# Ending the matrix memory inside the RWKV context features, and joining the features to the scan

## The chip, the core and the metric

The kernel runs on one core of a Trainium2 chip. The metric is device time in microseconds (us): the median of three runs of the kernel before is 2667.61 us (2666.59 to 2672.57).

## What is computed

One layer of a diffusion backbone: two token mixers on the same normalised input (a bidirectional RWKV-7 scan and a bidirectional chunkwise mLSTM, the "matrix memory"), a gated merge, and a PEER expert FFN. 512 latent tokens are computed, and 256 context tokens before them whose final states start the latent scans. The parts that the change touches:

```python
# mLSTM: the end of its output (both directions z, 4 heads of 128)
h = num / jnp.maximum(jnp.abs(den), jnp.exp(-m_row))[..., None]
h = h * rsqrt(mean(h * h, -1) + NORM_EPS) * mlstm_norm_g     # per head and direction
y = jnp.sum(h, axis=directions)
# RWKV: what the scan reads
decay = exp(-exp(w_log));  a = sigmoid(a0 + ad @ a_up)
kk = k * k_k / max(norm(k * k_k), 1e-12);  k_eff = k * (1 + (a - 1) * k_a)
S = S * w_t - s_kk (kk_t * a_t) + v_t k_t                    # 8 heads of 64 x 64
```

## The kernel before

The program is a row of blocks. Between two blocks all engines meet; inside one, every engine runs its own list of instructions, in the order in which they are written, and waits on semaphores. The blocks around the change, in order:

- `phase_mlstm` (the matrix memory): TensorE makes products per chunk of 128 tokens, ScalarE and VectorE gather them in `hc`. Its end handles the norms. VectorE makes the reciprocal of each denominator (L1746 to L1748, `den_done`), GpSimd multiplies the chunk by it (L1492, `divided`), ScalarE squares it (L1633), VectorE sums the squares (L1732). After the last of the eight, ScalarE makes Ln and Exp of all sums (L1654, L1656), GpSimd scales direction 1 (L1495, four times 128x512), VectorE scales direction 0 (L1754) and adds the two (L1757), TensorE turns the 16 tiles of 128x128 (L1606), and ScalarE and VectorE evict two heads each (L1659, L1760).
- `phase_rwkv_features` for the context (names ending in `_c`, 256 tokens), then later for the latent tokens (`_x`, 512 tokens). There are eight units n = (direction z, column tile c), four per direction. For each, TensorE makes two projections (`project`, L596 and L598), ScalarE makes the decay's tanh, the rate's tanh and the decay's exp (L569, L571, L577), for direction 1 also `ke` (L582; GpSimd makes it for direction 0, L615). VectorE makes a running product over each chunk of 64 with `tensor_tensor_scan` (`decay`, L638) and the rates (`rates`, L649). After unit 2, ScalarE also makes Ln and Exp of the four norms of `kk` (L586, L588). The decay buffer `w65` has 65 columns per chunk: direction 0 has its reset column in front and direction 1 behind, so VectorE rewrites it between the directions (L666), after the fourth scan, and ScalarE waits for that (`slot_done`) before the exp of the fifth unit.
- `phase_rwkv_scan`, again for the context and then for the latent tokens: a hardware loop over chunks of 64 tokens, the two directions g = 0 and 1 side by side. `prepare` on GpSimd makes `pr` (L772, L775), `ks` (L777) and, after VectorE's reciprocal `ginv` (`inverse`, L991), `qs` and `ks` (L782). The first products on TensorE (L915) read these: "Q0" and "Q1" below are those of the first chunk with `qs` of direction 0 and 1, 16 records each. VectorE's second reciprocal waits for GpSimd's first `prepare`, since the semaphore's count is started behind it (`start`, L69).

The order of the work is the order of the code; no planner decides anything. After the latent scan follow output, merge, routing and experts, which all begin behind a meeting of the engines.

In the text a "unit" is one of the eight of the features, counted from 1; "the last unit's end" is the end of L582 of unit 8.

Of the kernel before, what the change touches and what calls it, by code (L numbers as in the profile page):

```python
# [12 lines left out]
F32 = mybir.dt.float32  # L13
# [519 lines left out]
def phase_rwkv_features(nc, a, b, f, T, tag):  # L533

    nch = T // C
    with ExitStack() as ctx:
# [8 lines left out]
        w65 = sb("w65" + tag, [P, PAIRS, nch, C + 1])  # L545
        first = sb("w65_first" + tag, [P, nch, C + 1])
        tmp = sb("rw_tmp" + tag, [P, PAIRS, T])
        th = sb("rw_th" + tag, [P, 2, T])
        ps = [ctx.enter_context(nc.psum_tensor(f"ps_rf{k}" + tag, [P, 512], F32)) for k in range(4)]
        ps_n = [ctx.enter_context(nc.psum_tensor(f"ps_rn{k}" + tag, [P, 512], F32)) for k in range(PAIRS)]  # L550
# [4 lines left out]
        dve, scanned, slot_done, normed = sem("rwf_dve"), sem("rwf_scanned"), sem("rwf_slot"), sem("rwf_normed")  # L555
        line_pool, line_act = sem("rwf_line_pool"), sem("rwf_line_act")
        block = ctx.enter_context(nc.Block())
        units = [(z, c) for z in range(2) for c in range(PAIRS)]

        @block.scalar  # L560
        def _(act):
            act.activation(f[0:64, 12, :], f[0:64, 12, :], ACT.Tanh).then_inc(tanh_wd, 1)
            for c in range(PAIRS):
                act.wait_ge(sq_in, c + 1)
                act.activation(tmp[:, c, :], b.kk[:, c, 0:T], ACT.Square).then_inc(sq_done, 1)
            act.wait_ge(half_done, 1)
            for n, (z, c) in enumerate(units):
# [16 lines left out]
                if n == 1:  # L584
                    act.wait_ge(norm_max, 1)
                    act.activation(tmp[:], tmp[:], ACT.Ln).then_inc(norm_root, 1)  # L586
                    act.wait_ge(norm_root, 1)
                    act.activation(tmp[:], tmp[:], ACT.Exp, scale=-0.5).then_inc(norm_root, 1)  # L588

        @block.tensor  # L590
        def _(pe):
# [15 lines left out]
            for n in range(2, len(units)):  # L607
                project(n)

        @block.gpsimd  # L610
        def _(g):
            g.wait_ge(half_done, 1)
            for c in range(PAIRS):
                g.wait_ge(a_done, c + 1)
                g.tensor_scalar(b.ke[:, 0, c, 0:T], b.qa[:, 0, c, 0:T], ka[:, 0, c:c + 1], ka[:, 1, c:c + 1], ALU.mult,  # L615
                                ALU.add).then_inc(line_pool, 1)

        @block.vector
        def _(v):
# [8 lines left out]
            v.memset(w65[:, :, :, 0:1], 0.0).then_inc(slot_done, 1)  # L628

            def decay(n):  # L630
                z, c = units[n]
                v.wait_ge(dec_done, n + 1)
                w = w65[:, c].rearrange("p n t -> p (n t)")
# [17 lines left out]

            for c in range(PAIRS):
                v.wait_ge(norm_mm, c + 1)
                m = v.tensor_scalar(tmp[:, c, :], ps_n[c][:, 0:T], 1e-24, None, ALU.max)
# [10 lines left out]
            v.wait_ge(scanned, PAIRS)  # L665
            v.memset(w65[:, :, :, C:C + 1], 0.0).then_inc(slot_done, 1)  # L666
            v.wait_ge(slot_done, 2)
            for n in range(2, PAIRS):
                rates(n)
            for n in range(PAIRS, 2 * PAIRS):  # L670
                decay(n)
                rates(n)

def phase_rwkv_scan(nc, a, b, f, T, tag, need_out):
# [11 lines left out]
    with ExitStack() as ctx:  # L687
# [10 lines left out]
        pr, ginv = each("pr", [P, PAIRS, RW]), each("ginv", [P, PAIRS, C])  # L698

        pd, qs, ks, vs, lt, mt = (each(n, [P, PAIRS, C]) for n in ("pd", "qs", "ks", "vs", "lt", "mt"))  # L700
        qt, kt, ti, td, xd = (each(n, [P, PAIRS, C]) for n in ("qt", "kt", "ti", "td", "xd"))
        at, bt, vv, ro = (each(n, [P, PAIRS, C]) for n in ("at", "bt", "vv", "ro"))
        rr, uu, st, tm = (each(n, [P, PAIRS, C]) for n in ("rr", "uu", "st", "tm"))
# [18 lines left out]
        gi_s = [Steps(sem(f"rws_gi{g}"), ["gi"]) for g in range(2)]  # L722
# [3 lines left out]
        block = ctx.enter_context(nc.Block())  # L726
# [28 lines left out]
        def _(g_):  # L755
            def prepare(n, g, first=False):
# [2199 lines left out]
```

## Time and profile before

| | us |
|---|---|
| median of 3 runs | 2667.61 |
| the profiled execution, whole | 2667.66 |
| its span in the profile | 2665.9 |
| last instruction of the matrix memory ends | 332.73 |
| context features, first instruction to the last unit's end | 334.03 to 352.74 |
| context scan, "Q0" and "Q1" begin | 358.40, 362.14 |
| latent features, first instruction | 468.72 |
| latent scan, "Q0" and "Q1" begin | 504.09, 508.75 |

The profile is one execution. Its timeline has a row for an instruction or for a few equal ones in a row, with start, duration, engine, line, and in brackets the idle time of the engine before it and what ended it. Overlap is seen by comparing starts: an instruction on ScalarE or VectorE starts some 0.1 us before the one ahead of it has ended.

### The profile page before, as it was taken

What the parts mean: (1) busy time and instruction counts of PE and PEld (TensorE: products, weight loads), DVE (VectorE), ACT (ScalarE), POOL (GpSimd) and SP (SyncE); (2) the same over time, 40 slices, a digit from 0 to 9 for tenths busy, and PEclk for the clock granted to TensorE, in tenths of its full rate; (3) what the DMA queues carried; (4) which work ended last, traced back from release to release, by engine and by line L of the source; (5) the groups of instructions that cost most, each with busy time, mean ns of one, the idle gap of its engine ahead of it and who ended that gap; (6) DMA issues with size and microseconds to landing.
All of it is one profiled execution on the core that took longest, in us unless ns stands there. A gap on an engine that the chain in (4) does not pass through costs nothing.

```text
span 2665.9 us, 53106 instructions
## 1 busy us (share of the span) xinstructions
PE 2519.4 (95%) x19732; PEld 2078.4 (78%) x19732; DVE 1309.2 (49%) x2662; ACT 1020.5 (38%) x1725; POOL 850.1 (32%) x689
## 2 busy tenths in 40 slices
PE   7999669699999989999999999989999999999997
PEld 3885469499967867887888888878888888888886
DVE  5765655656553327997444444400044444444443
ACT  4222453533352233223666666632322322232222
POOL 2420243444554445645555555524400000000001
PEclk8999889799999999999999999999999999999999
DMA  6541000000032324234355444464455555555551
GB/s 263 188 174 40 1 2 1 2 0 0 1 145 89 94 71 143 85 100 144 115 205 181 169 169 169 169 236 142 134 196 197 190 189 189 191 196 196 194 197 64
DMA packets 163913, 348.64 MB, mean 131 GB/s; under 512 B 13368, under 2 KB 79416, under 8 KB 161664
## 3 DMA queue, kind: packets, MB, share of 16 engines
q1 hardware_dynamic: 163840, 347.65, 37.7%
q8 instruction: 48, 0.79, 0.1%
q14 instruction: 25, 0.20, 0.0%
HBM read 276.30 MB, written 71.30 MB: 130 GB/s over the span
## 4 chain that ended last, share of the span: by engine, by line
PE 53%; DVE 5%; issue 1%; DMA 1%; POOL 1%; ACT 1%; SPq 0%; DVEq 0%; ACTq 0%; POOLq 0%
PE ps_a L85 9%; PE ps_a L86 9%; PE ps_a L87 9%; PE ps_y L85 7%; PE ps_y L86 7%; PE ps_y L87 7%; PE ps_w L2535 4%; DVE cand L2328 0%; DVE top_ix L2311 0%; DMA w_scratch<-w_block 0%; DVE top_ix L2324 0%; DVE scores_left L2314 0%; DVE picked L2385 0%; DVE pick L2369 0%; DVE pick L2152 0%
## 5 line engine op out<-in xcount | busy, mean ns | idle before, releaser
L2711 DVE TENSOR_TENSOR v_lo<-v_raw,v_hi 128x1024 fp32r<-128x1024 f32 x128 | 158.3, 1237 | 542.2 <-ACT v_hi L2663 542.2
L85 PE MATMUL ps_a<-h_hi,u_hi 128*128 128x512 f32 x1024 | 412.0, 402 | 8.2 <-ACT act L2056 7.7
L86 PE MATMUL ps_a<-h_hi,u_lo 128*128 128x512 f32 x1024 | 405.7, 396 | 0.0
L87 PE MATMUL ps_a<-h_lo,u_hi 128*128 128x512 f32 x1024 | 405.7, 396 | 0.0
L2663 ACT ACTIVATE v_hi<-v_raw 128x1024 fp32r<-128x1024 f32 x128 | 135.8, 1061 | 478.4 <-PE ps_a L87 470.0
L85 PE MATMUL ps_y<-gated_hi,v_hi 128*128 128x512 f32 x768 | 299.5, 390 | 3.1 <-DVE gated_lo L2713 3.1
L87 PE MATMUL ps_y<-gated_lo,v_hi 128*128 128x512 f32 x768 | 299.3, 390 | 0.0
L86 PE MATMUL ps_y<-gated_hi,v_lo 128*128 128x512 f32 x768 | 299.2, 390 | 0.0
L2056 ACT ACTIVATE act<-ps_a 128x512 f32<-128x512 f32 x128 | 76.5, 597 | 414.0 <-PE ps_a L87 397.4
L85 PEld LDWEIGHTS ps_a<-h_hi,u_hi 128*128 128x128 f32 x1024 | 194.0, 189 | 52.4 <-issue 8.5
L2699 POOL TENSOR_TENSOR v_raw<-v_raw 128x512 f32<-128x512 f32 x6 | 7.7, 1288 | 711.7 <-ACT v_raw L2683 711.7
L87 PEld LDWEIGHTS ps_a<-h_lo,u_hi 128*128 128x128 f32 x1024 | 193.4, 189 | 46.0
L86 PEld LDWEIGHTS ps_a<-h_hi,u_lo 128*128 128x128 f32 x1024 | 193.9, 189 | 43.1
L2516 POOL TENSOR_SCALAR mixed<-iota,w_token 128x128 f32<-128x128 f32 x128 | 151.4, 1183 | 218.2 <-PE ps_w L2535 202.4
L2040 POOL TENSOR_TENSOR u_lo<-u_raw,u_hi 128x1024 fp32r<-128x1024 f32 x64 | 156.3, 2445 | 181.6 <-ACT u_hi L2036 181.6
L2040 DVE TENSOR_TENSOR u_lo<-u_raw,u_hi 128x1024 fp32r<-128x1024 f32 x64 | 78.5, 1226 | 251.4 <-ACT u_hi L2036 251.4
L85 PEld LDWEIGHTS ps_y<-gated_hi,v_hi 128*128 128x128 f32 x768 | 144.5, 188 | 33.5 <-DVE v_lo L2711 3.5
L87 PEld LDWEIGHTS ps_y<-gated_lo,v_hi 128*128 128x128 f32 x768 | 144.5, 188 | 30.1
L86 PEld LDWEIGHTS ps_y<-gated_hi,v_lo 128*128 128x128 f32 x768 | 144.5, 188 | 30.0
L2036 ACT ACTIVATE u_hi<-u_raw 128x1024 fp32r<-128x1024 f32 x128 | 134.4, 1050 | 40.8 <-DMA u_raw<-in_uT 40.8
L2567 ACT ACTIVATE w_block<-ps_w 128x512 f32 x128 | 141.2, 1103 | 0.0
L1077 POOL TENSOR_TENSOR mg_w_lo<-mg_raw,mg_w_hi 128x1024 fp32r<-128x1024 f32 x38 | 94.0, 2475 | 126.9 <-ACT mg_w_hi L1073 126.9
(524 smaller groups left out, 5417.4 us busy)
## 6 DMA issues: line engine op xcount, KB each, us to landing
u_raw<-in_uT SPq DMA_DIRECT2D x128, 512.0 KB, 3.6
v_raw<-in_v SPq DMA_DIRECT2D x128, 512.0 KB, 4.8
a_scratch<-act SPq DMA_DIRECT2D x128, 256.0 KB, 2.1
w_scratch<-w_block SPq DMA_DIRECT2D x8, 4096.0 KB, 12.2
w_ring<-w_scratch SPq DMA_DIRECT2D x64, 512.0 KB, 4.4
gated<-a_scratch SPq DMA_DIRECT2D x128, 256.0 KB, 4.8
mg_raw<-in_w_merge SPq DMA_DIRECT2D x36, 512.0 KB, 3.6
vM<-in_ada_rows SPq DMA_DIRECT2D x32, 512.0 KB, 4.9
```

The source lines that it names most:

```text
L85: pe.matmul(out, wh, xh, start=first, stop=False)
L86: pe.matmul(out, wl, xh, start=False, stop=False)
L87: return pe.matmul(out, wh, xl, start=False, stop=last)
L1077: g.tensor_tensor(self.wl[:, k], self.raw[:, k], self.wh[:, k], ALU.subtract).then_inc(self.w_lo, 1)
L2036: act.activation(self.uh[:, q], self.raw[:, q % 2], ACT.Copy).then_inc(self.hi, 1)
L2040: eng.tensor_tensor(self.ul[:, q], self.raw[:, q % 2], self.uh[:, q], ALU.subtract).then_inc(self.lo, 1)
L2056: act.activation(self.act[:, q % 2], self.ps[q % 2][:], ACT.Gelu).then_inc(self.out, 1)
L2516: g_.tensor_scalar(oi[:, s, SUB - 1], iota, cur[:, s, 0:1], cur[:, s, 1:2], ALU.is_equal, ALU.mult).then_inc(built_p, 1)
L2535: m = pe.matmul(ps[s][:, k, :], oi[:, s, k], oj[:, s, k], start=True, stop=True)
L2567: act.activation(wb[:, half, :, bass.ds(g * BODY + dt, SUB)].rearrange("p j t -> p t j"), ps[s][:], ACT.Copy).then_inc(evac[s], 1)
L2663: act.activation(vh[:, q], v_raw[:, q], ACT.Copy).then_inc(v_hi, 1)
L2711: v.tensor_tensor(vl[:, q], v_raw[:, q], vh[:, q], ALU.subtract).then_inc(v_lo, 1)
```

## The change

1. `phase_mlstm` ends after its last reciprocal. The last two divisions (GpSimd), the last two squares (ScalarE) and sums (VectorE), Ln and Exp, the scaling, the adding, the turning and the evictions are moved into the context features. There ScalarE, and no longer VectorE, scales direction 0, in 16 instructions of 128x128; GpSimd still scales direction 1.
2. `w65` exists once per direction, so no rewriting and no wait between the directions.
3. Features and scan are one block, for the context and for the latent tokens. The scan's first reciprocals become four small ones (128x64) per direction, made between the scans and rates of units 5 to 8. GpSimd's first `prepare` waits on the features' semaphores per direction, and "Q" waits for `qs` alone, where it waited for `ks` too.

```diff
 # phase_rwkv_features, ScalarE
+            if end is not None:
+                for z in range(2):
+                    act.wait_ge(end.divided, z + 1)
+                    act.activation(square[:, z], outer(z), ACT.Square).then_inc(end.squared, 1)
...
-                if z == 1:
-
-                    act.wait_ge(slot_done, 2)
-                act.activation(w65[:, c, :, 1:] if z == 0 else w65[:, c, :, 0:C],
+                act.activation(w65[0][:, c, :, 1:] if z == 0 else w65[1][:, c, :, 0:C],
...
                     act.activation(tmp[:], tmp[:], ACT.Ln).then_inc(norm_root, 1)
+                    if end is not None:
+                        act.wait_ge(end.reduced, 2)
+                        act.activation(end.ssq[:], end.ssq[:], ACT.Ln, bias=b.eps[:, 0:1], scale=1.0 / DV).then_inc(
+                            end.rooted, 1)
...
+                        for i in range(n_x):
+                            for h in range(MH):
+                                m = act.activation(y[:, 0, i, h * DV:(h + 1) * DV], hc[:, 0, i, h, 0:DV], ACT.Copy,
+                                                   scale=end.ssq[:, 0, i, h:h + 1])
+                            m.then_inc(end.scaled0, 1)
+                if n == PAIRS and end is not None:
+                    act.wait_ge(end.turned, 1)
+                    for h in range(MH // 2, MH):
+                        act.activation(b.yb[:, h, :].rearrange("p (r w) -> p w r", w=GRID_W),
+                                       ps_n[h][:].rearrange("p (w r) -> p w r", r=ROWS), ACT.Copy, scale=end.gain[:, h:h + 1])
 # TensorE
             for n in range(2, len(units)):
+                if n == PAIRS and end is not None:
+                    pe.wait_ge(norm_max, 1)
+                    for i in range(n_x):
+                        pe.wait_ge(end.summed, i + 1)
+                        for h in range(MH):
+                            mm = pe.transpose(ps_n[h][:, i * MC:(i + 1) * MC], y[:, 0, i, h * DV:(h + 1) * DV], b.ident[:])
+                    mm.then_inc(end.turned, 1)
                 project(n)
 # GpSimd
+                if c == 1 and end is not None:
+                    g.wait_ge(end.rooted, 2)
+                    g.wait_ge(end.divided, 2)
+                    for i in range(n_x):
+                        g.tensor_tensor(y[:, 1, i].rearrange("p (h v) -> p h v", v=DV), hc[:, 1, i, :, 0:DV],
+                                        end.ssq[:, 1, i].unsqueeze(2).to_broadcast([P, MH, DV]), ALU.mult).then_inc(
+                                            end.scaled1, 1)
 # VectorE
             for n in range(2, PAIRS):
                 decay(n)
-            v.wait_ge(scanned, PAIRS)
-            v.memset(w65[:, :, :, C:C + 1], 0.0).then_inc(slot_done, 1)
-            v.wait_ge(slot_done, 2)
             for n in range(2, PAIRS):
                 rates(n)
+            if end is not None:
+                for i in range(n_x):
+                    v.wait_ge(end.scaled0, i + 1)
+                    v.wait_ge(end.scaled1, i + 1)
+                    v.tensor_tensor(y[:, 0, i], y[:, 0, i], y[:, 1, i], ALU.add).then_inc(end.summed, 1)
...
             for n in range(PAIRS, 2 * PAIRS):
                 decay(n)
+                m = inverse(0, n - PAIRS)
...
                 rates(n)
+                if n == PAIRS and end is not None:
+                    v.wait_ge(end.turned, 1)
...
+                m = inverse(1, n - PAIRS)
...
 # phase_rwkv_scan, GpSimd, then TensorE
+                if first:
+                    g_.wait_ge(entry.scanned, (g + 1) * PAIRS)
+                    g_.wait_ge(entry.normed, (g + 1) * PAIRS)
+                    g_.wait_ge(entry.line_act if g else entry.line_pool, PAIRS)
...
+                        prep_s[g].wait(pe, i, "k" if k else "q")
                         if k == 0:
-                            prep_s[g].wait(pe, i, prep_names[-1])
```

What moves, in rows of each engine's list (line numbers are those of the kernel that is listed). TensorE, from the end of the matrix memory to the projections of the context's third unit, before:

```order
L1589 MATMUL ps_mu<-vM,ml_kw_x 64x129 x2
L1606 MATMUL ps_ms<-ident,mixed 128x128 x2
L1606 MATMUL ps_me<-ident,mixed 128x128 x2
L1431 UNCONDITIONAL_BRANCH
L590 UNCONDITIONAL_BRANCH
L596 MATMUL ps_rf_c<-fC,wa_up 128x256
L598 MATMUL ps_rf_c<-fC,wa_up 128x256
L606 MATMUL ps_rn_c<-rw_tmp_c,block_ones 128x256 x4
```

and in the changed kernel, from the norms of `kk` on:

```order
L648 MATMUL ps_rn_c<-rw_tmp_c,block_ones 128x256 x4
L638 MATMUL ps_rf_c<-fC,wa_up 128x256
L640 MATMUL ps_rf_c<-fC,wa_up 128x256
L655 MATMUL ps_rn_c<-ident,mixed 128x128 x16
L638 MATMUL ps_rf_c<-fC,wa_up 128x256
L640 MATMUL ps_rf_c<-fC,wa_up 128x256
```

The 16 turnings (four times the pair L1606 before, L655 now) stand between the projections of unit 4 and those of unit 5. VectorE, context features of the changed kernel, from the scans of units 3 and 4 on:

```order
L699 SCALAR_TENSOR_TENSOR G<-w_0_c,w_first_c 128x260 x2
L710 SCALAR_TENSOR_TENSOR qa<-qa,kk 128x256 x2
L736 TENSOR_TENSOR mixed<-mixed 128x512 x4
L699 SCALAR_TENSOR_TENSOR G<-w_1_c,w_first_c 128x260
L741 RECIPROCAL ginv<-G 128x64
L710 SCALAR_TENSOR_TENSOR qa<-qa,kk 128x256
L754 TENSOR_SCALAR mixed<-ps_rn_c,mlstm_g 128x64x8 x2
```

The four additions L736, on which the turnings wait, stand behind the rates (L710) of units 3 and 4. VectorE in the latent features, units 5 and 6, before:

```order
L666 MEMSET w_x 128x32
L649 SCALAR_TENSOR_TENSOR qa<-qa,kk 128x512 x2
L638 SCALAR_TENSOR_TENSOR G<-w_x,w_first_x 128x520
L649 SCALAR_TENSOR_TENSOR qa<-qa,kk 128x512
```

and now:

```order
L710 SCALAR_TENSOR_TENSOR qa<-qa,kk 128x512 x2
L699 SCALAR_TENSOR_TENSOR G<-w_1_x,w_first_x 128x520
L741 RECIPROCAL ginv<-G 128x64
L710 SCALAR_TENSOR_TENSOR qa<-qa,kk 128x512
```

Two small reciprocals stand in every one of the units 5 to 8, one behind the scan and one behind the rates, and the rewriting is gone.

## Rows read from the trace of the kernel before

**Rows 1.** Stretch 324 to 330 us: PE, PEld, DVE, ACT, POOL busy, PEclk, DMA.
```profile
324.00:330.00 6.00, 3.80 (x15) 2.60 (x15) 5.17 (x6) 0.00 (x0) 2.07 (x2) 0.50 0.00 0
```

**Rows 2.** Timeline, all engines, end of the matrix memory (start, us, instruction, idle before).
```profile
311.82 0.63 ACT L1625 ACTIVATE ml_hc<-ps_mi,g_cols 128x129 f32<-128x129 f32 x2 [0.96 <-PE ps_mu L1589]
...
314.86 0.18 DVE L1748 RECIPROCAL ml_dn<-ml_dn 128x4 f32<-128x4 f32 x1
...
322.29 1.44 DVE L1757 TENSOR_TENSOR mixed<-mixed 128x512 f32<-128x512 f32 x1 [1.00 <-POOL mixed L1495]
...
328.58 0.69 DVE L1757 TENSOR_TENSOR mixed<-mixed 128x512 f32<-128x512 f32 x1
...
330.48 2.25 ACT L1659 ACTIVATE mixed<-ps_me,mlstm_g 128x512 f32<-128x512 f32 x2 [9.92 <-PE ps_me L1606]
```

**Rows 3.** Timeline, all engines, context features.
```profile
334.03 0.42 ACT L562 ACTIVATE fC<-fC 64x256 f32<-64x256 f32 x1 [1.30 <-PEq L105]
...
334.44 1.34 ACT L565 ACTIVATE rw_tmp_c<-kk 128x256 f32<-128x256 f32 x4
...
339.75 1.06 ACT L586 ACTIVATE rw_tmp_c<-rw_tmp_c 128x1024 f32<-128x1024 f32 x1 [0.25 <-DVE rw_tmp_c L654]
...
343.08 0.46 ACT L569 ACTIVATE rw_th_c<-ps_rf_c,rw_half_c 128x256 f32<-128x256 f32 x1
...
345.12 1.75 POOL L615 TENSOR_SCALAR ke<-qa,rw_ka_c 128x256 f32<-128x256 f32 x1 [0.26 <-ACT qa L571]
...
345.31 0.48 ACT L569 ACTIVATE rw_th_c<-ps_rf_c,rw_half_c 128x256 f32<-128x256 f32 x1
...
346.86 0.76 DVE L649 SCALAR_TENSOR_TENSOR qa<-qa,kk 128x256 f32<-128x256 f32 x2
346.92 0.51 ACT L577 ACTIVATE w_c<-rw_th_c,eps 128x256 f32<-128x256 f32 x1 [0.77 <-DVE w_c L666]
...
352.14 0.60 ACT L582 ACTIVATE ke<-qa,rw_ka_c 128x256 f32<-128x256 f32 x1
```

**Rows 4.** Timeline of TensorE alone, the last turnings and a projection.
```profile
329.33 0.69 PE L1606 MATMUL ps_ms<-ident,mixed 128*128 128x128 f32 x2 [0.21 <-DVE mixed L1757]
329.81 0.64 PE L1606 MATMUL ps_me<-ident,mixed 128*128 128x128 f32 x2
...
346.20 0.79 PE L596 MATMUL ps_rf_c<-fC,wa_up 64*128 64x256 f32 x1
...
346.79 0.63 PE L596 MATMUL ps_rf_c<-fC,wa_up 64*128 64x256 f32 x1
```

**Rows 5.** Timelines of VectorE and of TensorE alone, start of the context scan.
```profile
354.50 1.75 DVE L991 RECIPROCAL ginv_c<-G 128x256 f32<-128x256 f32 x1
...
358.21 1.75 DVE L991 RECIPROCAL ginv_c<-G 128x256 f32<-128x256 f32 x1 [1.97 <-POOLq L69]
...
362.14 1.97 PE L915 MATMUL ps_rs_c<-pr_c,qs_c 64*64 64x128 f32 x16 [1.77 <-POOL ks_c L782]
```

**Rows 6.** Timelines of one engine each, latent features and start of the latent scan.
```profile
488.46 0.72 ACT L577 ACTIVATE w_x<-rw_th_x,eps 128x512 f32<-128x512 f32 x1 [2.35 <-DVE w_x L666]
...
488.40 1.29 DVE L649 SCALAR_TENSOR_TENSOR qa<-qa,kk 128x512 f32<-128x512 f32 x2
...
496.60 1.24 DVE L638 TENSOR_TENSOR_SCAN G<-w_x,w_first_x 128x520 f32<-128x520 f32 x1 [0.64 <-ACT w_x L577]
...
500.19 1.75 DVE L991 RECIPROCAL ginv_x<-G 128x256 f32<-128x256 f32 x1
...
508.75 2.82 PE L915 MATMUL ps_rs_x<-pr_x,qs_x 64*64 64x192 f32 x16 [1.84 <-POOL ks_x L782]
```

**Rows 7.** Groups by line and shape, whole span: xcount | busy us, mean ns | idle.
```profile
L2544 ACT ACTIVATE w_away<-iota,slots 128x128 f32<-128x128 f32 x132 | 52.2, 395 | 6.3 <-DMA iota<-in_iota 6.3
...
L2399 DVE RECIPROCAL soft_total<-soft_total 128x32 f32<-128x32 f32 x1 | 0.4, 353 | 0.0
```

**Rows 8.** TensorE's waits from 354 to 712 us: us in total, times, longest.
```profile
PE ps_rs_c L882 <- issue: 4.3, 6, 1.3
```

More of the change, by code:

```diff
@@ L530, in rwkv_masks, with __init__, sem, phase_rwkv_features @@
     return np.concatenate([out, out], 0)
-def phase_rwkv_features(nc, a, b, f, T, tag):
+class ScanEntry:
+    def __init__(self, nc, b, tag, ginv):
+        def sem(name):
+            return b.semaphore(nc, name + tag)
+        self.ginv = ginv
+        self.gi_s = [Steps(sem(f"rws_gi{g}"), ["gi"]) for g in range(2)]
+        self.scanned, self.normed = sem("rwf_scanned"), sem("rwf_normed")
+        self.line_pool, self.line_act = sem("rwf_line_pool"), sem("rwf_line_act")
+def phase_rwkv_features(nc, a, b, f, T, tag, block, entry, end=None):
     nch = T // C
@@ L611, in _ @@
         def _(g):
+            if end is not None:
+                for z in range(2):
+                    g.tensor_tensor(outer(z), outer(z), end.dn[:, z, chunk(z)].unsqueeze(2).to_broadcast([P, MH, DV]),
+                                    ALU.mult).then_inc(end.divided, 1)
             g.wait_ge(half_done, 1)
@@ L650, in rates @@
                                        op1=ALU.mult).then_inc(normed, 1)
+            if end is not None:
+                for z in range(2):
+                    v.wait_ge(end.squared, z + 1)
+                    v.tensor_reduce(end.ssq[:, z, chunk(z)], square[:, z], AX.X, ALU.add).then_inc(end.reduced, 1)
             for c in range(PAIRS):
@@ L697, in phase_rwkv_scan @@
         UN = RW - C
[L698 to L703, printed above, removed]
+        lt, mt, qt, kt, ti, td, xd = (each(n, [P, PAIRS, C]) for n in ("lt", "mt", "qt", "kt", "ti", "td", "xd"))
+        rr, uu, tm = (each(n, [P, PAIRS, C]) for n in ("rr", "uu", "tm"))
+        if need_out:
+            at, bt, vv = (each(n, [P, PAIRS, C]) for n in ("at", "bt", "vv"))
+        pd, qs, ks, vs, ro, st = (each(n, [P, PAIRS, C]) for n in ("pd", "qs", "ks", "vs", "ro", "st"))
+        pr, ginv = each("pr", [P, PAIRS, RW]), entry.ginv
+        if not need_out:
+            at, bt, vv = (each(n, [P, PAIRS, C]) for n in ("at", "bt", "vv"))
         lm = each("lm", [P, len(LEVELS), PAIRS, C])
@@ L991, in inverse @@
                 gi_s[g].mark(v.reciprocal(ginv[g][:], b.G[:, g, :, bass.ds(start_of(n, g, C + 1, 1 - g), C)]))
-            for g in range(2):
-                gi_s[g].start(v)
-                inverse(0, g)
             def body(i, more):
@@ L1411, in _, with __init__, place, sem @@
                               ps_t[k][:, 0:NCH * 2 * GROWS]).then_inc(cols_done, 1)
-def phase_mlstm(nc, a, b):
+class MemoryEnd:
+    def __init__(self, nc, ctx, b):
+        sb = alloc(nc, ctx)
+        self.ssq = sb("ml_ssq", [P, 2, TX // MC, MH])
+        self.dn = sb("ml_dn", [P, 2, TX // MC, MH])
+        self.gain = sb("mlstm_g", [P, MH])
+        self.hc = None
+    def place(self, nc, b):
+        def sem(name):
+            return b.semaphore(nc, name)
+        self.divided, self.squared, self.reduced, self.rooted = (sem(f"me_{n}") for n in ("div", "sq", "red", "root"))
+        self.scaled0, self.scaled1, self.summed, self.turned = (sem(f"me_{n}") for n in ("sc0", "sc1", "sum", "turned"))
+def phase_mlstm(nc, a, b, end):
     n_c, n_x = TC // MC, TX // MC
@@ L1487, in _ @@
             g.tensor_copy(neg_r[32:LOW], blank).then_inc(gaps, 1)
-            for n in range(2 * n_x):
+            for n in range(2 * n_x - 2):
                 i, z = n // 2, n % 2
@@ L2798, in build_program @@
             b.rwo_vecs = sm("rwo_vecs", [P, 3, PAIRS])
+            b.memory_end = MemoryEnd(nc, mixers, b)
             with ExitStack() as ml:
```

111 lines of the change are left out of this document (52 added, 59 removed).

## The prediction, made before the changed kernel was run

> **What bounds the kernel now.** I read the page first, for the span of 2665.9 us, then cut the first 520 us into stretches, and there read the timeline of each engine. The change touches only the blocks from the end of the matrix memory to the start of the latent scan, and every block begins where all engines have met, so a microsecond saved or lost in one of them moves all that follows by a microsecond. No data comes from HBM in this stretch (DMA share 0.00 in [rows 1], as in the stretches beside it), so nothing there gets later by starting earlier. In the stretch the reader should see a relay of engines, in which no engine is full. After the last reciprocal of the matrix memory at 315.04 (314.86 + 0.18) only the norms' relay runs, until the last eviction ends at 332.73 (330.48 + 2.25) [rows 2]. In the context features ScalarE is the one that hardly rests: from 334.03 to 352.74 it stands still for little more than 0.25 us before L586 and 0.77 us before the fifth unit's exp [rows 3]. The start of the scan is a relay again, of VectorE's two reciprocals, GpSimd and TensorE: from the end of the last unit, 352.74, to "Q1" at 362.14 it takes 9.4 us [rows 3, 5].
>
> **Part 1, the end of the matrix memory is taken off.** The block ends at 315.04 where it ended at 332.73 [rows 2]; the meeting behind it costs the same 1.3 us as now (332.73 to 334.03) [rows 3]. That is **-17.7 us**, and it is paid back in the next part. The two divisions that GpSimd gets at the block's start are hidden: ScalarE has its tanh and four squares first (1.75 us) [rows 3].
>
> **Part 2, the context features get longer.** ScalarE's chain decides. I count from the block's first instruction (334.03 before).
> - Two squares of 128x512 ahead of unit 1. By four squares of 128x256 in 1.34 us, 0.335 each [rows 3], two twice as wide take 1.05 us. 0.25 of it falls into the idle time before L586 [rows 3]: +0.8.
> - Ln and Exp on 32 columns, each below one of those squares: +0.4. The two table loads of the old tail need no payment, since these two stand beside the Ln and Exp of `kk`.
> - 16 scaled copies of 128x128 from SBUF. No row shows this form back to back. From below, half of a 128x256 square, 0.17 each [rows 3]; from above, L2544 of the same shape with 0.395 [rows 7], say 0.41 from start to start. The nearest is L1625, same operation with the same kind of scale, two in 0.63, so some 0.28 from start to start [rows 2]. 16 x 0.28 = +4.5.
> - Unit 3 then begins at 9.05 + 0.8 + 0.4 + 4.5 = 14.75 instead of 9.05 (343.08), and the two units end at 17.0, since two take 2.23 us (343.08 to 345.31) [rows 3].
> - **A new wait.** Unit 5 needs its projection, which stands on TensorE behind the 16 turnings; these need the four additions on VectorE, which stand behind the scan and the rates of unit 4. So after 17.0: the last scan 0.7 (half of 1.24 and the fixed part [rows 6]), two rates 0.8 [rows 3], 0.5 for GpSimd's last `ke`, which is late (1.75 us for it while VectorE scans [rows 3]), the first addition 0.7 [rows 2], 16 turnings at 0.24 (two in 0.48, from 329.33 to 329.81; the granted clock is 0.50, the 1.2 GHz level, in the stretch of the old ones, after TensorE's pause [rows 1, 4]) and 0.2 for the last: 4.1, and the projection 1.2 (346.20 to 347.42) [rows 4]. That is 8.0: unit 5 begins at 25.0 where it began at 11.3 (345.31) [rows 3], 13.7 later. ScalarE stands still for all 8.0 of it. GpSimd's four scalings (1.44 us each by the slowed L1757, of the same shape [rows 2]: 5.8) run beside the copies and the units 3 and 4 (6.7) and cost nothing.
> - Two evictions on ScalarE behind unit 5: +2.25 [rows 2]. The wait for the rewriting is gone: -0.77 [rows 3]. VectorE's two evictions and small reciprocals lie beside ScalarE's units.
>
> Sum of part 2: 13.7 + 2.25 - 0.77 = **+15.2 us**.
>
> **Part 3, the context scan starts earlier.** Now: last unit's end to "Q1" 9.4 us. Then: the last scan and its small reciprocal end 0.7 us after the last unit (the scan overlaps its `ke`). From the first reciprocal's end (354.50 + 1.75 = 356.25) to "Q1" it is 5.9 us now [rows 5]; they hold six steps of GpSimd, and 0.9 of it is the step of `ks` that "Q1" no longer waits for. The second reciprocal no longer waits for GpSimd (1.97 us idle [rows 5]) and is ready in time. 0.7 + 5.0 = 5.7: **-3.7 us**.
>
> **Part 4, the latent features and scan.** ScalarE no longer waits 2.35 us for the rewriting [rows 6], but that is not what comes back: VectorE becomes the one that ends last. It is through with the rates of unit 4 at 489.7 (488.40 + 1.29) as before. Each of the units 5 to 8 then costs it a scan 1.15 and rates 0.6 [rows 6] and two reciprocals of 64 columns. The reciprocal is bounded by 32 columns in 0.353 [rows 7] and by half of 256 columns, 0.88 [rows 6]; a line through both full rows gives 0.55, or 0.47 from start to start. A unit is then 2.7 us, where ScalarE needs 2.46. The last reciprocal of direction 0 ends at 489.7 + 3 x 2.7 + 1.15 + 0.55 = 499.5. From the first reciprocal's end at 501.94 to "Q1" at 508.75 it is 6.8 us [rows 6], less 0.9 for `ks`: "Q1" at 505.4: **-3.3 us**.
>
> **The sum.** -17.7 + 15.2 - 3.7 - 3.3 = -9.5 us. Against the profiled execution of 2667.66 us, which is the median of the runs within 0.1 us, that is **2658.2 us**. The loops of both scans, and all that follows, I cost at nothing: their instructions are the same.
>
> **A rule weighed.** GpSimd now makes three steps of the latent `prepare` beside VectorE's chain of part 4; seven such steps stand in 6.8 us now [rows 6], so three are 2.9. The trace shows both outcomes for such a pair: L1757 took 1.44 us beside GpSimd and 0.69 without [rows 2], and L615 took 1.75 us beside two scans that kept their pace [rows 3]. So the sum has VectorE unhindered. The Trainium skill (SBUF — State Buffer, "Who interferes with whom") says that a VectorE instruction with two SBUF inputs contends with a GpSimd instruction that reads SBUF, and that the loser blocks for the whole instruction. By that VectorE could lose all 2.9.
>
> **The rivals.**
> - *The larger gain.* TensorE is granted full speed during the turnings. They then follow the additions: 3 x 0.6 + 0.5 instead of 4.1, and a projection 0.5 shorter, -2.3; with copies at 0.17, -1.8. Together -13.6: 2654.1. Against it stands the clock of 0.50 in the old turnings [rows 1]. 0.13.
> - *VectorE loses the port* to GpSimd three times in the latent features: +2.9, so -6.6: 2661.1. 0.10.
> - *The join does nothing.* If GpSimd starts `prepare` only when all of VectorE's list is through, parts 3 and 4 give nothing: -2.5: 2665.2. For it: the waits are on counts that the last units fill. Against it: direction 0 needs only the first four. 0.06.
> - *All dear ends.* Copies at 0.41 (+2.1), reciprocals at 0.88 (+2.3 for seven), port (+2.9): -2.2; with the most of each about -4: 2663.7. 0.06.
> - *Slower.* In the first pass of the context scan's loop TensorE stands still with nothing to wait for, up to 1.3 us at a time; with the code behind the loop it is 4.3 us in six places [rows 8], and none of them is in a later pass, so it looks like the price of code that runs for the first time. The join puts the loops at other places of the code. Should the pause come back in every pass, there are 2 + 6 more passes, at most 8 x 4.3 = 34 us, so +25: 2693. It decides from the third such pass on. The rows speak against it, since later passes have no such pause. 0.05.
>
> **How the numbers follow.** My forecast has 0.60. What a measurement of this kernel can tell from no change is about 0.2%, 5.3 us, so up to 2662.3 is faster. Faster: 0.60 + 0.13 + 0.10 = 0.83; within 0.2%: 0.06 + 0.06 = 0.12; slower: 0.05. The unknown costs are copies (-1.8, +2.1), clock (-2.3, 0), reciprocals (-1.4, +2.3) and port (0, +2.9); as independent they make -3.2 and +4.3. With the spread of the runs I take 2654.0 to 2662.8, which leaves out the last three rivals, 0.17.
>
> **What would show it right or wrong.** The matrix memory's last instruction near 315.0. ScalarE idle for some 8 us before the fifth unit's first tanh, released by TensorE, and TensorE in turn released by the additions (L736 of the rows above). The context's last unit ending near 350, "Q1" some 5.7 us later. In the latent features VectorE without idle time from unit 5 on, and "Q1" 36.7 us after the block's first instruction, where it is 40.0 now. Wrong would be: ScalarE's idle time below 5 or above 11 us, the small reciprocals above 0.8 us, pauses of TensorE in later passes, or a change of the time behind the latent scan.

## The result, and the profile after

| | before | changed |
|---|---|---|
| median of 4 runs each | 2670.09 us | 2725.99 us |
| lowest to highest | 2666.59 to 2672.59 | 2724.59 to 2731.74 |
| profiled execution, time (span) | 2667.66 (2665.9) | 2724.59 (2722.8) |

The ratio is 1.0214, with a 95% interval of 1.0193 to 1.0235: slower by 56 us. The forecast was 2658.2 us and the range ended at 2662.8. Nearly all of the time went where I had written zero.

First the part that was forecast. ScalarE's timeline of the changed kernel in the context features, the counterpart of [rows 3] (start, us, instruction, idle before and its releaser):

```profile
316.81 0.42 ACT L585 ACTIVATE fC<-fC 64x256 f32<-64x256 f32 x1 [3.37 <-PEq L105]
...
319.09 1.03 ACT L588 ACTIVATE rw_tmp_c<-kk 128x256 f32<-128x256 f32 x3 [0.63 <-DVE kk L682]
...
328.50 4.78 ACT L623 ACTIVATE mixed<-ml_hc,ml_ssq 128x128 f32<-128x128 f32 x16
...
343.06 0.47 ACT L596 ACTIVATE rw_th_c<-ps_rf_c,rw_half_c 128x256 f32<-128x256 f32 x1 [7.55 <-PE ps_rf_c L640]
...
344.68 2.02 ACT L629 ACTIVATE mixed<-ps_rn_c,mlstm_g 128x512 f32<-128x512 f32 x2
...
350.76 0.65 ACT L606 ACTIVATE ke<-qa,rw_ka_c 128x256 f32<-128x256 f32 x1
```

TensorE's timelines of the same kernel, for the turnings, "Q1" of the context scan, and three passes of the latent scan's loop (a pass begins with the product that reads `qs`; the counterparts are [rows 4 to 6]):

```profile
337.71 4.15 PE L655 MATMUL ps_rn_c<-ident,mixed 128*128 128x128 f32 x16 [13.29 <-DVE mixed L736]
...
357.57 1.97 PE L1006 MATMUL ps_rs_c<-pr_c,qs_c 64*64 64x128 f32 x16 [1.84 <-POOL qs_c L874]
...
499.78 1.58 PE L1006 MATMUL ps_rs_x<-pr_x,qs_x 64*64 64x192 f32 x16 [1.97 <-POOL qs_x L874]
...
538.85 4.38 PE L1006 MATMUL ps_rs_x<-pr_x,qs_x 64*64 64x192 f32 x32 [6.58 <-issue]
...
578.74 4.91 PE L1006 MATMUL ps_rs_x<-pr_x,qs_x 64*64 64x192 f32 x32 [6.53 <-issue]
...
619.23 5.14 PE L1006 MATMUL ps_rs_x<-pr_x,qs_x 64*64 64x192 f32 x32 [6.87 <-issue]
```

Up to "Q1" of the latent scan all goes as forecast: 499.78 where it was 508.75 [rows 6], 9.0 us ahead. Then the lead turns into a loss. The same loop in the kernel before, on TensorE's timeline:

```profile
541.22 2.82 PE L915 MATMUL ps_rs_x<-pr_x,qs_x 64*64 64x192 f32 x32
...
570.43 2.82 PE L915 MATMUL ps_rs_x<-pr_x,qs_x 64*64 64x192 f32 x32
```

A pass took 29.2 us (570.43 - 541.22) and now takes 40.5 (619.23 - 578.74). The loop is left for the last pass, which stands behind it in the code, at 776.7; from "Q1" to there it is 276.9 us. In the kernel before it was 716.10 - 508.75 = 207.4. The difference, 69.5, less the lead of 9.0, is 60.5; the spans differ by 56.9, so 3.6 come back further on, which is within what executions of this kernel differ by.

One pass, cut out of each kernel (stretch, length, TensorE busy, granted clock, share of the DMA engines, GB/s). The changed one:

```profile
578.74:619.23 40.49, 31.58 (x832) 0.92 0.02 4
```

and the one before:

```profile
570.43:599.60 29.17, 28.76 (x832) 1.00 0.00 0
```

The same 416 products, 832 records in each. Of the 11.3 us, 8.5 are idle time of TensorE (8.9 against 0.4), and 2.8 are slower products. These follow the pause. The granted clock of the changed kernel right behind a pause of 6.5 us, at the end of the products on `qs`, and 6 us into the pass:

```profile
578.80:581.00 2.20, 2.20 (x14) 0.50 0.03 7
582.00:584.00 2.00, 2.00 (x22) 0.74 0.00 0
585.00:600.00 15.00, 14.37 (x447) 1.00 0.01 3
```

So TensorE stands still, is granted 1.2 GHz when it begins again, and gets the 2.4 GHz back within the first products: 4.91 us for 32 records that took 2.82.

What does it wait for? Nothing that an engine does. TensorE's waits from 495 to 800 us in the changed kernel (us in total, times, longest):

```profile
PE ps_rs_x L1006 <- issue: 39.3, 6, 6.9
...
PE ps_rs_x L991 <- issue: 9.9, 14, 1.3
PE ps_rs_x L974 <- issue: 5.5, 10, 0.9
```

and from 500 us in the kernel before:

```profile
PE ps_rs_x L882 <- issue: 2.4, 6, 0.8
PE ps_ro L1152 <- PEq L105: 2.1, 1, 2.1
PE ps_rs_x L899 <- issue: 1.0, 2, 0.8
```

The DMA queues name a suspect. The line of the instruction queue in the page before, over the whole span (packets, MB, share):

```profile
q8 instruction: 48, 0.79, 0.1%
```

in the page after:

```profile
q8 instruction: 102, 1.67, 0.3%
```

and in the changed kernel between 542 and 583 us, one pass:

```profile
q8 instruction: 9, 0.15, 1.5%
```

### The profile page after: what moved, and what is told of

Same layout as the page of the kernel before. It is cut to its first block, busy times and chain, and to the rows that moved or that the text cites. A ratio compares the mean times of both kernels' runs of the same rounds, so it can differ in the third digit from the quotient of the medians.

```text
span 2722.8 us, 53105 instructions
## 1 busy us (share of the span) xinstructions
PE 2531.0 (93%) x19732; PEld 2087.1 (77%) x19732; DVE 1307.7 (48%) x2670; ACT 1021.2 (38%) x1739; POOL 845.7 (31%) x689
## 4 chain that ended last, share of the span: by engine, by line
PE 51%; DVE 5%; issue 1%; DMA 1%; POOL 1%; ACT 1%; SPq 0%; DVEq 0%; ACTq 0%; POOLq 0%
PE ps_a L85 9%; PE ps_a L86 9%; PE ps_a L87 9%; PE ps_y L85 6%; PE ps_y L86 6%; PE ps_y L87 6%; PE ps_w L2601 4%; DVE cand L2394 0%; DVE top_ix L2377 0%; DMA w_scratch<-w_block 0%; DVE top_ix L2390 0%; DVE scores_left L2380 0%; DVE picked L2451 0%; DVE pick L2435 0%; DVE pick L2218 0%
## 5 line engine op out<-in xcount | busy, mean ns | idle before, releaser
L2601 PEld LDWEIGHTS ps_w<-mixed 128*128 128x128 f32 x1024 | 125.7, 194 | 10.2 <-POOL mixed L2582 4.8
```

What stands on the lines that cost most here:

```text
L2601: m = pe.matmul(ps[s][:, k, :], oi[:, s, k], oj[:, s, k], start=True, stop=True)
```

## The experiments

Twelve kernels. "Counting instructions" are `pe.sem_inc` on a semaphore that nobody waits for. Beside them the kernel before had a median of 2668.04 us (2668.67 for the second group, those with the parts of the change, the better version and the 252 instructions). Those without a ratio are single runs, enough for differences of tens of us.

### Four instructions ahead of the loop

```diff
+            if tag == "_x":
+                for _ in range(4):
+                    pe.sem_inc(padded, 1)
             pe.wait_ge(tanh_wd, 1)
```

> The changed kernel with four TensorE instructions put in ahead of the latent scan's loop, each of which only counts up a semaphore that nobody waits for. Counted in the program, they put the first instruction of that loop's body back to the number that it has in the kernel before (4817 of TensorE's own, against 4813 in the changed one; the body has 1729). Theory A, placement: TensorE's instructions come in blocks of 256 (16.4 KB packets of the instruction queue); the body of 1729 covers 7 blocks from the old place and 8 from the new one, with the block that is fetched ahead 8 against 9, and 9 no longer fit, so that each pass fetches all of them again (54 packets more in the trace, 9 for each of 6 passes). With the four instructions the time falls by about 65 us to 2658 to 2664, the instruction queue shows about 48 packets, not 102, the pass takes 29.2 us, not 40.8, and no product of Q shows a pause of issue from the second pass on. Theory B, the change itself (one block for features and scan, the wait for q alone, the memory of the buffers) makes TensorE stand still: four instructions that do nothing leave the time at 2720 to 2732 and the packets at about 102.

Measured: 2660.65 us (8 runs, 2655.45 to 2667.01), ratio to before 0.9969 (0.9955 to 0.9982). The page and TensorE's timeline of this kernel:

```profile
q8 instruction: 48, 0.79, 0.1%
```

```profile
530.72 2.82 PE L1010 MATMUL ps_rs_x<-pr_x,qs_x 64*64 64x192 f32 x32
...
559.89 2.82 PE L1010 MATMUL ps_rs_x<-pr_x,qs_x 64*64 64x192 f32 x32
```

Passes of 29.2 us, 48 packets, no pause. Four instructions that do nothing take away 65 us. All of the change is in this kernel, so theory B falls, and the time is what the change is worth without the accident: 7.4 us less than before by the medians and 8.3 by the ratio, whose interval goes from 4.8 to 12.0, where the sum had said 9.5.

### Behind the loop, far ahead of it, and two in place of four

The same four put behind the loop; put into the context's features, some 3100 instructions further ahead; and two at the first place.

> A control: the changed kernel with the four counting instructions behind the latent scan's loop instead of ahead of it. Placement: the loop's body lies where it lay in the changed kernel, so 2722 to 2735 us and 102 packets. If four instructions anywhere do it (another alignment of what follows): 2655 to 2667 us.

> A control: the changed kernel with the four counting instructions some 3100 TensorE instructions further ahead, in the context's features, and none in the latent ones. Placement: 2655 to 2667 us and 48 packets, as with the four close to the loop, since only the count ahead of the body matters. If the instructions had worked by a delay at the place where they stood: 2720 to 2732 us, 102 packets.

> The changed kernel with two counting instructions ahead of the loop, not four. The border of a block lies between the two starts, four instructions apart; this tells in which half. Placement allows two results only: about 2660 us with 48 packets, or about 2726 us with 102 (then the body of the kernel before begins on the first or second instruction of its block). A gradual effect would show a time in the middle, about 2690 us.

Measured: 2733.79, 2656.91 and 2660.72 us, with 102, 48 and 48 packets. So only the count ahead of the body matters, not where a delay stands, and not what follows the loop. With two the loop is whole again: the border lies between the starts 4813 and 4815. There is no middle.

### The kernel before, pushed along

None of the change is in these: the counting instructions go into the kernel before.

> The same with 56 counting instructions. Theory A: 56 + 3 + 1729 = 1788 still ends within the seventh block: 2665 to 2675 us and about 48 packets, in spite of only twelve instructions fewer than in the other kernel. A rival to it, that any shift of the loop by tens of instructions is harmful, or that the added instructions themselves cost the time: slow as the one with 68.

> The kernel before, none of the change in it, with 68 such counting instructions ahead of the latent scan's loop. Theory A: the loop's body starts 68 later; if the old start is 0 to 3 instructions behind the border of a block (it must be, if four fewer put it across), the body now ends behind the seventh block (68 + 1729 = 1797, over 7 x 256 = 1792), covers 8 blocks, and the kernel before becomes slow too: about 2667 + 65, 2725 to 2740 us, about 102 packets. Theory B: nothing of the change is in it, 2665 to 2675 us, 48 packets.

> The kernel before with 252 counting instructions ahead of the latent scan's loop: its body then begins at the same place within a block of 256 as in the changed kernel, 4 short of where it was. The instructions cost 0.18 us each in the kernels with 56, 68 and 100 of them, 45 us here. Theory of placement: six passes fetch all of the body again, 54 packets more (102), 65 us more on top: about 2668 + 45 + 65 = 2778 us. If the change itself were needed for the loss: about 2713 us and 48 packets. A third way, that distance and not place within a block decides, would show a few refetched passes as with 100 (four of them): 84 packets, about 2755.

> The kernel before with 160 counting instructions. The body reaches 97 to 100 instructions into an eighth block; it reached 5 to 8 into it with 68 (one pass fetched again, 9 packets), 33 to 36 with 100 in the changed kernel (four passes, 36 packets) and 189 to 192 with 252 (six, 55 packets). If the block fetched ahead (the ninth) needs time, and the branch back to the start calls it off when it comes early, the number of passes that are fetched again rises with the reach: 5 or 6 passes here, 93 to 102 packets, and 2668 + 28 for the instructions + 55 to 65 = 2751 to 2761 us. If the number is chance: anything between one pass and six.

And the changed kernel with 100:

> The changed kernel with 100 counting instructions in the place of four. Theory A: the body starts 96 to 99 behind the border, 99 + 1729 = 1828 is over 1792, eight blocks again: 2720 to 2735 us, about 102 packets, passes of 40.8 us. A rival, that the changed kernel only wanted some delay on TensorE ahead of the loop, or that its loop must not begin at a block's last instructions but may begin anywhere else: 2658 to 2668 us and 48 packets.

The expectations for 56, 68 and 100 left out the price of the counting instructions, 0.16 to 0.18 us each, which the trace shows as one pause of issue ahead of the latent projections. The table takes it off. The reach is how far the body goes into an eighth block. It needs the exact border, and TensorE's instruction records give it. In the kernel before with 252, the branch back at 623.03 us takes 3.6 us (0.2 where nothing is fetched), three instructions of the body run, and the fourth comes 3.0 us later. In the changed kernel the branch at 571.48 also takes 3.6 us, but only one instruction runs before the next wait of 3.3 us. The second wait is that for the second block, so the body begins on the third-last instruction of a block with 252, and on the last one in the changed kernel. In the kernel before, the start is 252 instructions earlier, which within a block of 256 is the same as four later: the second instruction of a block, two later than in the changed kernel.

| kernel | us | packets | price of the added, us | us without them | passes fetched again | reach into the 8th block |
|---|---|---|---|---|---|---|
| before, 56 | 2681.30 | 48 | 10.3 | 2671.0 | 0 | none |
| before, 68 | 2680.72 | 57 | 12.1 | 2668.6 | 1 | 6 |
| changed, 100 | 2709.08 | 84 | 17.1 | 2692.0 | 4 | 36 |
| before, 160 | 2740.27 | 102 | 26.4 | 2713.9 | 6 | 98 |
| before, 252 | 2773.96 | 103 | 40.5 | 2733.5 | 6 | 190 |

The changed kernel itself has a reach of 192. The one packet that the kernel with 252 has above 102 lies outside these six passes, which have nine each; its program is one block longer.

TensorE's waits of the kernel before with 252, two of its latent part (the first is the price of the added instructions):

```profile
PE ps_rf_x L597 <- issue: 40.5, 1, 40.5
PE ps_rs_x L919 <- issue: 37.8, 6, 6.5
```

and of the one with 160:

```profile
PE ps_rf_x L597 <- issue: 26.4, 1, 26.4
PE ps_rs_x L919 <- issue: 25.3, 6, 4.3
```

and one pass of the kernel before with 68, the only one that pauses (its neighbours last 29.2 us):

```profile
641.16 4.50 PE L919 MATMUL ps_rs_x<-pr_x,qs_x 64*64 64x192 f32 x32 [4.49 <-issue]
```

The kernel before, with its loop moved to within two instructions of where the changed kernel has it, loses 64.8 us (2733.5 against 2668.7), where the changed one loses 65.3 (2726.0 against 2660.7). That settles the cause from the other side. But theory A as I had first put it was too coarse: an eighth block alone costs little. The branch back is taken six times. With a reach of 6 the body is fetched again after one of them (nine packets), with 36 after four, from 98 on after all six. The expectation of 2725 to 2740 us for the kernel with 68 was wrong by its bare time of 2668.6, and that of 2720 to 2735 for the changed one with 100 by its 2692.0. A body on eight blocks fits, then: in the other five passes with 68, and the other two with 100, not one packet moves. What throws it out must be a ninth block, fetched ahead, and the times of the packets bear this out. Each pass that is fetched again has one packet ahead of those of its own eight blocks. It starts 0.8 to 1.1 us before the branch back in the changed kernel and with 252, and 0.1 to 0.6 us behind it with 160, 100 and 68; the passes without it fetch nothing. What starts this fetch, and why it comes in some passes and not in others of the same kernel, no row shows.

The kernel with 160 was also under its expectation, since the pause itself has two sizes: up to 4.5 us with 68, 100 and 160, up to 6.9 with 252 and in the changed kernel. In the latter two the body begins with the last three instructions or the last one of a block, so that TensorE waits for two blocks one behind the other, as the two waits told above show. With 68, 100 and 160 the branch alone waits, 4.2 to 4.7 us, and then the first products run without a second wait.

### The parts of the change, with the loop in its place

Features and scan in two blocks again, the end of the matrix memory left in the context's features (the loop begins six instructions later than before, within the seven blocks):

```diff
                     phase_rwkv_features(nc, a, b, b.fC, TC, "_c", block, entry, b.memory_end)
+                with nc.Block() as block:
                     phase_rwkv_scan(nc, a, b, b.fC, TC, "_c", False, block, entry)
```

and likewise for the latent tokens.

> The changed kernel with the four counting instructions, and features and scan of each phase in a block of their own again (with the barrier between them), the end of the matrix memory still inside the context's features; the loop of the latent scan then begins six instructions behind its place in the kernel before, within the range that the theory of placement calls harmless. Theory by the sum of the prediction: the earlier starts of both scans (3.7 and 3.3 us) are given back, 2660.7 + 7 = 2667.7 us. Rival: the join gave nothing and the moved end of the matrix memory gave all of the measured gain: 2660 to 2662.

Measured: 2668.27 us (11 runs), ratio 0.9993 (0.9981 to 1.0006), against 0.9969 with one block: 6.4 us given back, 7.0 expected. The two intervals only just meet, but the profiled executions agree: from the last context unit's end to "Q1" it is 9.3 us in two blocks and 6.2 in one, and from the latent block's start to "Q1" 41.6 against 37.4, 7.4 in all. The join is worth what parts 3 and 4 said, and the moved end of the matrix memory by itself is worth nothing that can be measured (-17.7 + 15.2 = -2.5 forecast, -1.9 by the ratio, whose interval takes in zero).

> The changed kernel with five counting instructions (the loop's body then begins where it did before), in which TensorE waits ahead of the products of Q for the last preparation again instead of for q alone. Theory by the prediction: only the first pass of each scan waits for POOL there, so it costs at most the 1.1 us of one multiplication of k in each of two phases: 2661 to 2663 us. Rival: the wait matters in every pass, 14 of them, 1 us each: 2670 to 2675.

Measured: 2661.52 us (10 runs), ratio 0.9969 (0.9957 to 0.9981), the same as without. TensorE waits 6.05 instead of 5.16 us ahead of the context's first product, and 11.4 instead of 10.5 ahead of the latent one, so the 0.9 us is there; it is too small to be seen in the time. In later passes the preparation is long done.

### A better version

The wait of 7.55 us on ScalarE is one of order on VectorE: its additions stand behind scans and rates that must first be waited for.

```diff
             for n in range(2):
                 decay(n)
+            for n in range(2):
+                inverse(0, n)
...
             for n in range(2):
                 rates(n)
+            if end is not None:
+                for i in range(n_x):
+                    v.wait_ge(end.scaled0, i + 1)
+                    v.wait_ge(end.scaled1, i + 1)
+                    v.tensor_tensor(y[:, 0, i], y[:, 0, i], y[:, 1, i], ALU.add).then_inc(end.summed, 1)
             for n in range(2, PAIRS):
                 decay(n)
             for n in range(2, PAIRS):
                 rates(n)
-            if end is not None:
...
+            for n in range(2, PAIRS):
+                m = inverse(0, n)
+            entry.gi_s[0].mark(m)
             for n in range(PAIRS, 2 * PAIRS):
                 decay(n)
-                m = inverse(0, n - PAIRS)
...
```

> The changed kernel with the four counting instructions, and VectorE's work in the features in another order: the four additions of the matrix memory stand right behind the rates of the first two units instead of behind those of the fourth, and the reciprocals of the first direction right behind the scans that they read instead of among the units of the second direction. What is computed stays the same. Theory: the 7.6 us that ScalarE stood still ahead of its fifth unit go, since the turnings then begin when POOL's last product is ready (333.9 us) and not behind the scans and rates of units three and four; VectorE's last stretch loses four reciprocals of 0.45 us net each in both phases, and POOL can prepare the first direction before VectorE is through with the second. The first product of the context scan's second direction comes about 8 us earlier and that of the latent scan about 3.6 us more: 2649 us, 11 to 12 us under the kernel with the four instructions alone. Rival: VectorE or POOL bounds the stretch anyway (VectorE has 14.5 us of work behind 333 us in the context), and only 3 to 6 us come: 2655 to 2658.

Measured: 2650.61 us (6 runs, 2641.25 to 2662.71), ratio 0.9934 (0.9910 to 0.9958), the fastest of all: 9.3 us under the kernel with four instructions by the ratios, 11.6 expected. ScalarE's timeline of this kernel:

```profile
322.67 0.42 ACT L586 ACTIVATE fC<-fC 64x256 f32<-64x256 f32 x1 [3.37 <-PEq L105]
...
344.79 0.47 ACT L597 ACTIVATE rw_th_c<-ps_rf_c,rw_half_c 128x256 f32<-128x256 f32 x1 [3.42 <-PE ps_rf_c L641]
```

and TensorE's:

```profile
339.41 1.09 PE L659 MATMUL ps_rn_c<-ident,mixed 128*128 128x128 f32 x4 [9.79 <-DVE mixed L745]
...
356.65 1.91 PE L1011 MATMUL ps_rs_c<-pr_c,qs_c 64*64 64x128 f32 x16 [0.38 <-POOL qs_c L879]
```

This execution came to the block 5.9 us later than that of the changed kernel (322.67 against 316.81), by something ahead of all that was edited, so I count from the block's first instruction. "Q1" comes after 34.0 us, 40.8 with the old order: -6.8, where I had expected 8. ScalarE still waits 3.4 us, not zero, since the 16 turnings run at a granted clock of 0.50 (339 to 343.5 us) and the projection stands behind them. In the latent features it is 34.7 against 37.4 us: -2.7, where I had expected 3.6. The two make 9.5, near the 9.3 of the ratios.

## Why the prediction was wrong

**The step that failed** is the last sentence of the sum: "The loops of both scans, and all that follows, I cost at nothing: their instructions are the same." They are, but not their places. The latent loop costs 11.3 us more in a steady pass and 69.5 in all. Pauses of TensorE in later passes stood in the prediction as a sign of being wrong, and they came. For the context's loop the zero held: its body of 1537 or 1538 instructions touches seven blocks from its place in either kernel.

**The rival with the right mechanism** was "slower": TensorE stands still in every pass, since "the join puts the loops at other places of the code". It said +25, 2693 us, "at most 8 x 4.3 = 34 us", and had 0.05. Two things were off. The size: [rows 8] gave 4.3 us for the whole first pass, and I took this as the price of fetching a loop. But in the first pass the blocks come ahead of their use; in a pass that must fetch again the first two blocks are waited for in full (3.6 and 3.3 us, of which 6.5 count as idle), later ones in part (up to 1.3 us each), and the clock takes another 2.8. The chance: I wrote that "the rows speak against it, since later passes have no such pause". That was evidence on the kernel before, whose loop lies on seven blocks, and said nothing of one that begins a few instructions earlier. What would have told of the danger lay in reach without a run: the 48 packets of the instruction queue, the 1729 instructions of the body, and the difference ahead of it. From these the two starts could not be said to straddle a border. A body of 1729 lies on seven blocks from the first 64 places of a block alone, so a shift of four back leads over the border from 4 of 64, of two back from 2: an estimate of 0.03 to 0.06, if any of these places was as likely. The 0.05 was thus no bad number, though the reason given for it was a bad one. That this change met the border is bad luck: had the body begun one instruction further on in the kernel before, the same change would have been some 7 us faster. What was wrong is to cost a shift of a loop at nothing, and a price that was not that of a pass that is fetched again.

**The sum, term by term,** held to about a microsecond each:

| term | forecast | measured | from |
|---|---|---|---|
| 1, start of the context features | -17.7 | -17.2 | 316.81 against 334.03 |
| 2, length of the context features | +15.2 | +15.9 | 34.6 (351.41 - 316.81) against 18.7 |
| of it: 16 copies | 4.5 | 4.8 | L623 |
| of it: ScalarE ahead of unit 5 | 8.0 | 7.55 | L596 |
| of it: two evictions | 2.25 | 2.02 | L629 |
| 3, last unit to "Q1" | -3.7 | -3.2 | 6.2 (357.57 - 351.41) against 9.4 |
| 4, latent block to "Q1" | -3.3 | -3.7 | 36.3 against 40.0 |

What part 2 missed is 1.44 us in which ScalarE waits for VectorE's `kk` between the squares at the block's start (0.63 of it in the row of L588); it was not there before. The four terms make -9.5 as forecast and -8.2 as measured; the context scan gives 0.7 more (105.9 us from its "Q1" to the latent block's start, against 106.6), which makes the -9.0 at "Q1" of the latent scan. By the medians with the four instructions it is -7.4.

**The other rivals.** The turnings were granted 0.50 of the clock, as in [rows 1], so the larger gain did not come. The join does something, 6.4 us. Of the port the latent block says: part 4 came out 0.4 us better than forecast with three steps of GpSimd beside VectorE's chain, so nothing near 2.9 us was lost. But the two did hinder each other; the one that lost was GpSimd. Its timeline in the changed kernel:

```profile
484.28 1.50 POOL L864 TENSOR_TENSOR pr_x<-kk,G 128x256 f32<-128x256 f32 x1 [2.44 <-DVE qa L710]
485.95 0.87 POOL L867 TENSOR_TENSOR pr_x<-fX,G 128x256 f32<-128x256 f32 x1 [0.18 <-POOL pr_x L864]
487.00 1.44 POOL L869 TENSOR_TENSOR ks_x<-ke,fX 128x256 f32<-128x256 f32 x1 [0.18 <-POOL pr_x L867]
493.70 0.95 POOL L874 TENSOR_TENSOR qs_x<-qa,ginv 128x256 f32<-128x256 f32 x1 [5.27 <-DVE ginv L741]
```

and of the same three steps in the kernel before, where they stand behind VectorE's units:

```profile
498.97 0.73 POOL L772 TENSOR_TENSOR pr_x<-kk,G 128x256 f32<-128x256 f32 x1 [11.88 <-SPq L687]
499.88 0.67 POOL L775 TENSOR_TENSOR pr_x<-fX,G 128x256 f32<-128x256 f32 x1 [0.18 <-POOL pr_x L772]
500.72 0.73 POOL L777 TENSOR_TENSOR ks_x<-ke,fX 128x256 f32<-128x256 f32 x1 [0.18 <-POOL pr_x L775]
```

The three take 3.8 us against 2.1, while VectorE's scans beside them take 1.21 and 1.23 us and those after them 1.17. By the rule of the Trainium skill (SBUF — State Buffer, "Who interferes with whom") VectorE could have lost all of the 2.9. The trace agrees that such a pair is slowed, but here it cost the other engine 1.7 us, and that was free, since GpSimd then waits 5.27 us for `ginv`.

## What to carry to other kernels

"Its instructions are the same" is no reason to cost a loop at nothing. Where a loop's body comes near what the engine's instruction memory holds, count the instructions of the body and those ahead of it in both programs, in the code that is loaded; an edit anywhere ahead can move it over a border, in either direction, and the number of packets in the instruction queue inside the loop tells at once. When a change brings a loss far from where it was made, try first to put the old place back with a few empty instructions: what is left over is the change's own worth.

## What the runs showed of the hardware that was not expected

- TensorE runs a loop on seven blocks of 256 instructions without fetching anything after the first pass. The Trainium skill (Runtime: NRT & Kernel Launch, "Instruction fetch mechanics") says that only two such blocks are held and that a branch out of them must wait for a fetch. Here the branch goes back 1729 instructions, and no packet moves between 545 and 660 us in the kernel before: the measurement decides, for TensorE. Its figure of room for 2048 instructions agrees with the eight blocks: a body that touches eight also runs passes without a packet (five of six with 68, two of six with 100).
- With nine blocks in play all nine are fetched in each pass, 16.4 KB each: 8.5 us of idle time and 2.8 of lower clock in 40.5 us.
- The further the body reaches into the eighth block, the more passes are fetched again (none, 1, 4, 6, 6 for none, 6, 36, 98, 190 instructions, one profiled execution each).
- A branch back to a block that had to be fetched took 3.3 to 3.8 us in the changed kernel and the one with 252, and the second block, needed at once, another 2.8 to 3.6; with 68, 100 and 160 the branch alone took 4.2 to 4.7.
- Where GpSimd and VectorE slow each other it can be GpSimd that pays: 3.8 us for three steps that take 2.1 alone.
- An instruction on TensorE that only counts up a semaphore takes 0.16 to 0.18 us when many stand in a row.
